# Probabilities turned in 32x32 blocks by VectorE and carried to their partitions by GpSimd's transfers through DRAM, in a two-layer hybrid diffusion backbone

## The reference

```python
h = modulate(rms_norm(x, g_mix[l]), sh1, sc1)          # hc: the same for the context tokens
a_b, a_c, a_x, na_q, na_k, na_v, sw_q, sw_k, sw_v, ga, gb, gc = split_in(h @ w_in[l])
o_a = a_b * short_conv(a_c * a_x, conv_w[l])
o_b = neighbourhood_attention(...)                     # 8 heads of 64, keys: latent + context, bias rpb
o_c = window_attention(...)                            # 8 query heads, 2 key heads, rotary, sink
x = x + gt1 * merge_branches((o_a, o_b, o_c), (ga, gb, gc), w_branch[l], w_out[l])
x = x + gt2 * expert_choice_ffn(modulate(rms_norm(x, g_ffn[l]), sh2, sc2), ...)   # 16 experts of 1024
```

## Time and profile before

| what | value |
|---|---|
| median of 3 runs | 1846.57 us (1845.81 to 1846.89) |
| span of the profiled execution | 1846.3 us |
| busy: PE, DVE, ACT, POOL | 1689.6, 771.0, 478.0, 111.4 us |
| mean granted TensorE clock | 0.976 |
| HBM read, written | 539.13 MB, 2.98 MB |

### The profile page before, as it was taken

The page is one execution under the profiler, slowest core; times in us unless marked ns, Lnnn a source line. Parts: engine busy times, 40 slices in busy tenths (PEclk is TensorE's granted clock), DMA queues, the critical chain, the costliest instruction groups (busy, mean ns, idle before and its releaser), DMA issues.

```text
span 1846.3 us, 26514 instructions
## 1 busy us (share of the span) xinstructions
PE 1689.6 (92%) x10854; PEld 977.2 (53%) x10854; DVE 771.0 (42%) x1746; ACT 478.0 (26%) x1052; POOL 111.4 (6%) x149
## 2 busy tenths in 40 slices
PE   5999999999998999999898799989999997777866
PEld 2887777777674333333232398877883332222222
DVE  3455556674434233333323665577753222111111
ACT  3324455552223100000000434465441000000001
POOL 1001210000001000000000101300001000000000
PEclk8999999999998999999999999999998999999998
DMA  9532322127778999999999764337899999999996
GB/s 353 154 91 69 106 72 80 35 81 256 251 286 326 409 428 427 428 428 428 427 429 426 271 206 133 96 115 252 282 364 385 426 426 426 426 425 426 426 426 281
DMA packets 152035, 543.83 MB, mean 295 GB/s; under 512 B 10026, under 2 KB 92400, under 8 KB 126700
## 3 DMA queue, kind: packets, MB, share of 16 engines
q1 hardware_dynamic: 149104, 535.35, 74.0%
q0 software_dynamic: 2400, 6.16, 1.2%
q10 hardware_dynamic: 412, 0.64, 0.1%
HBM read 539.13 MB, written 2.98 MB: 294 GB/s over the span
## 4 chain that ended last, share of the span: by engine, by line
PE 68%; DMA 23%; DVE 4%; ACT 2%; SPq 2%; issue 1%; POOL 0%; DVEq 0%; ACTq 0%
PE bank L2158 20%; PE bank L2019 12%; PE bank L2020 11%; PE bank L2021 11%; DMA ring<-in_w_exp_down 8%; DMA ring<-in_w_exp_gate 7%; DMA ring<-in_w_exp_up 4%; DMA spare<-in_w_exp_gate 3%; PE bank L2132 2%; PE bank L2048 2%; PE bank L2071 2%; PE bank L1934 2%; PE bank L2058 2%; PE bank L2187 1%; DMA ring<-in_w_ada 1%
## 5 line engine op out<-in xcount | busy, mean ns | idle before, releaser
L2158 PE MATMUL bank<-ring,XEP 128*32 128x256 f32 (+1 forms) x2384 | 384.9, 617 | 37.1 <-DMA ring<-in_w_exp_gate 20.7
L2019 PE MATMUL bank<-HH,WH 128*128 128x512 f32 (+1 forms) x864 | 312.1, 361 | 5.7 <-DVE HL L1627 4.7
L2020 PE MATMUL bank<-HL,WH 128*128 128x512 f32 (+1 forms) x864 | 300.4, 348 | 0.0
L2021 PE MATMUL bank<-HH,WL 128*128 128x512 f32 (+1 forms) x864 | 299.9, 347 | 0.0
L2158 PEld LDWEIGHTS bank<-ring,XEP 128*32 128x32 f32 (+1 forms) x2384 | 114.1, 130 | 277.5 <-issue 227.8
L1598 DVE TENSOR_TENSOR WL<-ring,WH 128x1024 fp32r<-128x1024 f32 (+1 forms) x172 | 185.0, 1078 | 133.4 <-ACT WH L1362 132.6
L1856 DVE TENSOR_TENSOR X<-X,bank 128x512 f32<-128x512 f32 x184 | 114.0, 682 | 188.2 <-PE bank L2187 100.0
L2019 PEld LDWEIGHTS bank<-HH,WH 128*128 128x128 f32 x864 | 163.8, 190 | 54.0 <-issue 25.9
L1362 ACT CAST WH<-ring 128x1024 fp32r<-128x1024 f32 (+1 forms) x172 | 158.0, 926 | 100.5 <-PE bank L2021 64.7
L2158 PE MATMUL bank<-ring,HIDT 128*32 128x256 f32 (+1 forms) x1232 | 153.6, 481 | 31.3 <-DMA ring<-in_w_exp_down 31.3
L2021 PEld LDWEIGHTS bank<-HH,WL 128*128 128x128 f32 x864 | 163.8, 190 | 21.2
(11 more groups left out here) (244 smaller groups left out, 1955.4 us busy)
## 6 DMA issues: line engine op xcount, KB each, us to landing
ring<-in_w_exp_gate SPq DMA_DIRECT2D x55, 2048.0 KB, 30.9
ring<-in_w_exp_up SPq DMA_DIRECT2D x49, 2048.0 KB, 34.4
ring<-in_w_exp_down SPq DMA_DIRECT2D x48, 2048.0 KB, 36.6
ring<-in_w_ada SPq DMA_DIRECT2D x48, 1024.0 KB, 7.4
ring<-in_w_in SPq DMA_DIRECT2D x40, 1024.0 KB, 6.3
split_slot<-in_w_exp_up SPq DMA_DIRECT2D x8, 2048.0 KB, 29.3
split_slot<-in_w_exp_down SPq DMA_DIRECT2D x8, 2048.0 KB, 33.5
ring<-in_w_in SPq DMA_DIRECT2D x28, 512.0 KB, 5.2
```

The source lines that it names most:

```text
L2019: mm(t, wh, hi[:, k, 0:b.n], start=k == 0, stop=False)
L2020: mm(t, wh, lo[:, k, 0:b.n], start=False, stop=False)
L2021: last = mm(t, wl, hi[:, k, 0:b.n], start=False, stop=k == b.kk - 1)
L2158: last = mm(out_bank[tw * g:tw * g + tw, 0:nw], stationary(k), w[:, g::G] if spread else w[:, nw * g:nw * g + nw], start=k == 0, stop=k == ...
```

## The change

TensorE's transposes of the probabilities and ScalarE's copies of them are gone, and the banks `TB` are not used any more. In their place:

- VectorE, right after it has normalised a unit, waits for its own result and turns `PB` in blocks of 32x32 into a tile `PBT` (one for both heads of a pair, at the end of the streaming ring). Ahead of the first head it waits until the pair before has left `PBT`.
- GpSimd, per pair, writes `PBT` to one of two DRAM buffers, waits for that write, waits for the values that last read the target, and issues four reads, each of which brings one quarter of the columns to 32 partitions of `PTL` or `PTC`, now in another order of dimensions.
- The streaming ring is 1,024 elements shorter while attention runs.
- Values run two pairs after the last pair of their set in layer 0 (at 0.4 of the pair's k-steps) and one pair after it in layer 1 (at 0.8). In stage C the first `dpair` has its steps in another order, with the last values further in.
- The bias steps of GpSimd are put in another place: a first one (layer 0) or two (layer 1) pairs' worth ahead, then one pair's worth, four transfers and two masks, behind each turn of a pair that has a bias.

The core of the diff:

```diff
+PBT_W = 1024
@@ def load
-            if self.top + size > STREAM[self.layer] * SLOT:
+            if self.top + size > STREAM[self.layer] * SLOT - self.kept:
@@ def attention
-                at_ = sorted(at_ + [(-(-per * 3 // 10), values), (-(-per * 7 // 10), lower)], key=lambda a: a[0])
+                at_ = sorted(at_ + [(-(-per * (8 if last else 4) // 10), lambda: values(pair[0].pair - (1 if last else 2))), (-(-per * (10 if last else 8) // 10), lower)], key=lambda a: a[0])
@@ values, turn
-            for st in P.turned:
-                P.add("pv", set=st)
-            P.lower += P.turned
-            P.turned = []
+            while P.turned and P.turned[0].end <= until + 1:
+                P.add("pv", set=P.turned[0])
+                P.lower.append(P.turned.pop(0))
-            for x in pair:
-                P.add("turn", unit=x)
-                if x.end:
-                    P.turned.append(x.set)
+            P.add("turn", pair=pair)
+            if pair[1].end:
+                P.turned.append(pair[1].set)
@@ stage C, for d2 in range(4)
-            run(atoms[:1 + KD // 2])
-            values()
-            run(atoms[1 + KD // 2:1 + KD])
-            lower()
-            run(atoms[1 + KD:mid])
+            if d2 == 0:
+                mid = 2 * KD + 3
+                atoms = atoms[:KD + 2] + atoms[KD + 8:2 * KD + 9] + atoms[KD + 2:KD + 8] + atoms[2 * KD + 9:]
+                done = 0
+                for n in (KD + 1, 2 * KD)[-len(P.turned):]:
+                    run(atoms[done:n])
+                    values(P.turned[0].end - 1)
+                    run(atoms[n:n + 3])
+                    lower()
+                    done = n + 3
+                run(atoms[done:mid])
+            else:
+                run(atoms[:mid])
@@ after the plan of a layer
-        P.steps[l] = out
+        P.steps[l] = bias_order(out, 2 * (l + 1))
+def bias_order(steps, ahead):
+
+    due = [s for s in steps if s.kind == "bias"]
+    out = []
+
+    def pair():
+
+        now = [due.pop(0) for _ in range(2)] if due else []
+        out.extend(now + [Step(kind="mask", layer=s.layer, unit=s.unit) for s in now])
+
+    for s in steps:
+        if s.kind == "bias":
+            if s.unit.u == min(t.unit.u for t in steps if t.kind == "bias"):
+                for _ in range(ahead // 2):
+                    pair()
+            continue
+        out.append(s)
+        if s.kind == "turn" and s.pair[0].bias:
+            pair()
+    assert not due
+    return out
@@ buffers
+        bounce = [nc.dram_tensor(f"bounce{i}", (128, PBT_W), f32, kind="Internal").ap() for i in range(2)]
-        PTL = sb("PTL", [128, 2, 4, SEQ], R_PT)
-        PTC = sb("PTC", [128, 2, 2, SEQ], R_PT + 8192)
+        PTL = sb("PTL", [128, 8, 2, 4, 32], R_PT)
+        PTC = sb("PTC", [128, 8, 2, 2, 32], R_PT + 8192)
+        PBT = [[sb(f"PBT{l}{nk}", [128, 4, 2, nk, 32], R_RING + 16384 * STREAM[l] - 4 * PBT_W) for nk in (4, 2)] for l in range(DEPTH)]
@@ gpsimd
+                    elif s.kind == "mask":
+                        mask(s.unit)
+                    elif s.kind == "turn":
+                        x = s.pair[1]
+                        pool.wait_ge(turn_ready, x.u + 1)
+                        run, held = 16 * x.nk // 32, bounce[x.pair % 2]
+                        if x.pair > 1:
+                            pool.wait_ge(pt_in, 64 * (x.pair - 1))
+                        pool.dma_start(held[:, 0:4 * run], PBT[l][x.set.grp][:].rearrange("p b h c j -> p (b h c j)")).then_inc(pt_out, 16)
+                        pool.wait_ge(pt_out, 16 * (x.pair + 1))
+                        if x.set.pt_before:
+                            pool.wait_ge(pv_ready, x.set.pt_before)
+                        j = x.qt % 2
+                        for b in range(4):
+                            blocks = bass.AP(tensor=held.tensor, offset=held.offset + run * b, ap=[[PBT_W, 32], [32 * PBT_W, 4], [1, run]])
+                            turned = (PTL, PTC)[x.set.grp][32 * b:32 * b + 32, 4 * j:4 * j + 4].rearrange("p a h c j -> p a (h c j)")
+                            pool.dma_start(turned, blocks).then_inc(pt_in, 16)
@@ scalar
-                    elif kind == "turn":
-                        x = s.unit
-                        act.wait_ge(turn_ready, x.u + 1)
-                        if x.set.pt_before:
-                            act.wait_ge(pv_ready, x.set.pt_before)
-                        nc.scalar.copy(buf[:, x.hh, :, 128 * j:128 * j + 128],
-                                       TB[x.u % 2][:, 0:128 * nk].rearrange("p (k q) -> p k q", k=nk)).then_inc(pt_ready, 1)
@@ vector, after the scaling
+                        dve.wait_ge(norm_ready, x.u + 1)
+                        if x.hh == 0 and x.pair:
+                            dve.wait_ge(pt_out, 16 * x.pair)
+                        turned = PBT[l][x.set.grp][:, :, x.hh, :, :].rearrange("p b c j -> p c b j")
+                        nc.vector.transpose(turned, PB[u2][:, 0:n].rearrange("p (c b j) -> p c b j", b=4, j=32)).then_inc(turn_ready, 1)
@@ tensor
-                    elif kind == "turn":
-                        x = s.unit
-                        pe.wait_ge(norm_ready, x.u + 1)
-                        if x.u >= 2:
-                            pe.wait_ge(pt_ready, x.u - 1)
-                        for c in range(x.nk // 128):
-                            last = nc.tensor.transpose(TB[x.u % 2][:, 128 * c:128 * c + 128], PB[x.u % 2][:, 128 * c:128 * c + 128], IDENT)
-                        last.then_inc(turn_ready, 1)
@@ tensor, values
-                        pe.wait_ge(pt_ready, st.end)
+                        pe.wait_ge(pt_in, 64 * st.end)
-                                last = mm(PVB[64 * hh:64 * hh + 64, 0:SEQ], v, buf[:, hh, c, :], start=c == 0, stop=c == n - 1,
+                                last = mm(PVB[64 * hh:64 * hh + 64, 0:SEQ], v, buf[:, :, hh, c, :], start=c == 0, stop=c == n - 1,
```

More of the change, by code:

```diff
@@ L205, in __init__ @@
         self.occupants = []
-        self.units = self.sets = self.biases = 0
+        self.units = self.sets = self.biases = self.pairs = 0
+        self.kept = 0
         self.mods = 0
@@ L502, in open_tile @@
             b.tile = P.tile(**kw)
+        P.kept = PBT_W
         ch = col_chunk("nv")
@@ L556, in attention @@
                     pair = []
+                    n = P.pairs
+                    P.pairs += 1
                     for hh in range(2):
                         x = Step(br=br, p=p, hh=hh, qt=2 * st.grp + j, u=P.units, info=info, nk=TOK if st.grp == 0 else CTX, set=st,
-                                 end=hh == 1 and j == 1, bias=None, layer=l)
+                                 end=hh == 1 and j == 1, bias=None, layer=l, pair=n)
                         P.units += 1
-                        st.end = P.units
+                        st.end = P.pairs
                         if br == "na" and x.qt < 2:
```

27 lines of the change are left out of this document (6 added, 21 removed).

## The result

| kernel | median of runs | span profiled | granted clock |
|---|---|---|---|
| before | 1846.2 us (4 runs, 1843.4 to 1846.9) | 1846.3 us | 0.976 |
| after | 1901.9 us (4 runs, 1894.6 to 1903.4) | 1901.6 us | 0.956 |

The ratio is 1.0296, with a 95% interval from 1.0276 to 1.0315. The forecast was 1822 us and its range ended at 1852. It went the way of rival (b), which had 0.18, and further than the 1865 us priced there.

The account below looks back on a forecast made before the run. Attention was taken as bound by TensorE, the expert stage by the weight stream. Terms of 10 + 9 + 5 + 4 - 2 = 26 us gave 1820.6 us, put at 1822, with a range of 1802 to 1852.

Parts of the forecast that it names:

- rival (b): na branches: GpSimd's serial chain sets the periods; landings longer by 1.5 us cost 44.5 us, giving 1865; chance 0.18.
- sw: 6.3 a pair, 11.8 a double, hidden in both layers: Window branches: the turn holds GpSimd 6.3 us a pair, 11.8 per large and small pair, and costs no time.
- a chain of 9.3: Each large pair: 9.3 us from the end of VectorE's transpose to the landed last read, 6.3 + about 3.
- the co-bound: Layer 1 sw: VectorE at 9.5 us a pair against TensorE's 9.6, so 4 us gained of a possible 8.8.
- wrong, if writes land in over 5 us: GpSimd's bounce writes: expected at 3 to 4.5 us; landings over 5 us would mean a slower kernel.
- both medians: Argument against slower na periods: bias landings had medians of 2.4 us in layer 0 and 2.9 in layer 1.
- Values of layer 0 come 14 to 15 us after it: Layer 0: values come 14 to 15 us after VectorE's transpose, so 5 us are spare.
- the later values at a loss of 2 us, and the ring at nothing: Layer 1's last values ten k-steps later, with two expert loads: -2 us; shorter ring delays some loads, costing nothing.
- layer 1's 15.5 + 7: Layer 1, TensorE's ceiling: 15.5 us of transposes and 7 us of waits for the probabilities go.
- Rival (d): Layer 1: weight stream, already held by its rate, ends when it did despite shorter TensorE work; 1843 to 1847; chance 0.07.
- (a): Whole kernel: nothing stalls, TensorE keeps 44 to 46 us, 1801; chance 0.2.
- the signs named: Profile: VectorE over 90% in layer 1 sw; TensorE idle ahead of values in layer 1 na, nowhere in layer 0 sw.

Follow-up runs that it names:

- e12: The kernel before without TensorE's transposes and ScalarE's copies, values computed from a tile filled with zeros once a layer: 1809.2 us, ratio 0.9795.
- e15: e12 with the streaming ring shorter: 1812.3 us, ratio 0.9815 to the kernel before.
- e5: The changed kernel without the transfers and without VectorE's transposes, values waiting for the scaled probabilities: 1824.9 us, ratio 0.9888 to the kernel before.
- e3: The changed kernel without the transfers; values wait for VectorE's transposes alone and read a zero-filled tile: 1831.7 us, ratio 0.9930 to the kernel before.
- e13: e3 with all bytes of the bounce moved, reads fetching other data into DRAM, values not waiting for them: 1842.8 us, ratio 0.9977 to the kernel before.
- e9: The change in layer 0 alone, with the last head pair of the window branch left to TensorE: 1839.3 us, ratio 0.9960 to the kernel before.
- e6: The kernel before with the streaming ring 1,024 elements shorter during attention, nothing else: 1848.7 us, ratio 1.0016.
- e16: e12 with the values one or two pairs later, as in the changed plan: 1824.3 us, ratio 0.9871 to the kernel before.
- e11: The changed kernel with layer 1's modulation weights for its first nine chunks cut to an eighth: 1887.0 us, ratio 1.0224 to the kernel before.

## Why the prediction was wrong

Put one behind the other, the medians account for the whole way:

| step | us | predicted |
|---|---|---|
| turns and copies away (before to e12) | -36.7 | -46.5 |
| shorter ring (e15) | +3.1 | 0 |
| values later, and the plan around them (e5) | +12.6 | 2 |
| VectorE's transposes (e3) | +6.8 | 8 |
| the bytes alone (e13) | +11.1 | 0 |
| the waits for them (after) | +59.1 | 11 |
| sum | +56 | -26 |

(The predicted column sorts the prediction's terms: VectorE was to eat 3 us in layer 0's sw and 4.8 in layer 1's, GpSimd 2 in layer 0's na and some 9 in layer 1's na. Its sum is 26 within rounding.)

By stage, from the profiled executions, against the terms of the prediction's sum (na from the first na score to the first sw score, sw from first to last score; minus is faster; the last column is what the waits for the transfers added):

| stage | predicted | before to after | e13 to after |
|---|---|---|---|
| layer 0 na | -10 | -7.4 | +5.4 |
| layer 0 sw | -9 | -1.3 | +7.2 |
| layer 0 hand-over | 0 | +15.5 | +14.3 |
| layer 1 na | -5 | +10.7 | +14.1 |
| layer 1 sw | -4 | +31.9 | +20.9 |
| layer 1 hand-over | +2 | +6.8 | +3.4 |
| sum | -26 | +56.2 | +65.3 |

**The step that failed: "sw: 6.3 a pair, 11.8 a double, hidden in both layers".** It set the time that the turn holds GpSimd against the period of a pair, a question of rate. What the window branch needs is a question of delay: by the prediction's own count the values come 1.1 pairs after the transpose, and at the 9.6 us wanted per pair that is 10.6 us against a chain of 9.3, the same one to two us of slack as in layer 1's na, for which alone it was worked out. The 9.3 was too short as well, in layer 1 by 3 to 4 us. From the end of VectorE's second transpose of a pair to its last landed read the trace has, in the median of each branch, 10.3 and 9.6 us in layer 0 (na, sw) and 12.8 and 13.4 in layer 1; the eight pairs of layer 1's sw lie between 8.8 and 16.6, seven of them over 11.

Not all of the 31.9 us there are this wait. Without any transfer the branch was already longer than before: from first to last score it took 74.7 us before, 68.9 without turns (e12), 73.1 with the shorter ring (e15), 77.5 with the later values (e5), 82.8 with VectorE's transposes (e3), 85.7 with the bytes (e13) and 106.6 in the change. So the saving of 4 us was lost before the waits came on top. Nor was VectorE the co-bound that the prediction made of it (9.5 of 9.6 us a pair): in e3 it was busy 71.7 of 89.2 us there, 80%, and TensorE idled 11.1 us. 11.6 us of TensorE's idle in all of e3 are the wait for `QT` shown above, which no term of the prediction has.

**Second: the chain had medians in it, and the engine that waits pays the tails.** The values wait for one write and then for the slowest of four reads. The write was assumed at 3.8 us and measured at 3.6, so "wrong, if writes land in over 5 us" was the wrong test: the median never did. But writes took up to 8.8 us and reads up to 7.8, and a wait is not regained where TensorE is the bound. Rival (b) had the longer landings right. It priced a mean delay d over the time that GpSimd is held in layer 0's na, where the large writes landed in 2.9 us in the median, and in layer 1's na; the window branches and the hand-over of layer 0, where 42 of the 65 us between e13 and the change are, are not in it. Its own argument against itself, "both medians", was what misled.

**Third: what a stall does besides.** TensorE's direct waits for reads are 41.8 us, the cost of waiting 59.1. The profiled executions of e13 and of the change lie 65.5 us apart. The sums over all stretches from the first score to the first gather of both layers hold 65.3 of them, e13 first, then the change (us, then busy times):

```profile
sum 698.60, PE 658.84 PEld 498.99 DVE 472.45 ACT 283.13 POOL 204.12; mean PE 131.77 PEld 99.80 DVE 94.49 ACT 56.63 POOL 40.82
```
```profile
sum 763.90, PE 679.37 PEld 507.40 DVE 472.41 ACT 282.89 POOL 199.41; mean PE 135.87 PEld 101.48 DVE 94.48 ACT 56.58 POOL 39.88
```

TensorE idled 84.5 us instead of 39.8, 44.8 more, nearly all of it the direct waits. And the same matmuls kept it busy 20.5 us longer: the granted clock was 0.85 in the window branch of layer 1 instead of 0.94, and 0.93 in layer 0's hand-over instead of 0.98. Eight sets of sixteen values matmuls behind waits took 3.06 to 3.68 us instead of 1.95; they are 13 of the 20.5, and the other products have the rest. The prediction had no such term, since the clock stood at 1.00 in all stretches of the earlier trace rows. Two waits of other engines for the same chain are in the trace too: in the window branch of layer 1 GpSimd twice waited, 14.7 us in all, for the values to leave the single `PTL`, and VectorE waited 20.8 us over the whole kernel for `PBT`, 17.7 of them in layer 0.

**Fourth: the hand-over of layer 0.** "Values of layer 0 come 14 to 15 us after it": within attention 12.6 us were lost against e13 all the same (255.8 against 243.2). One reason shows in GpSimd's timeline: its bias steps stood ahead of them in the queue, and so four of the first sixteen writes began 5 to 10 us after VectorE's transposes. At its end there is no next pair, SP had loads of 1 MB under way, and the write landed after 8.84 us. The hand-over cost 14.3 us more than without the waits (190.4 against 176.1), and e9 does not have this loss.

**Fifth: the later values at a loss of 2 us, and the ring at nothing.** The ring costs 3 (by twelve runs of e6; the 3 of e15 alone are within the noise). The move costs 7 us with the turns in place and 12 to 15 without. In layer 0 it is all in the hand-over (172.7 to 179.2), where the order of the steps changed; 5.1 us of these 6.5 are TensorE's busy time, 165.1 to 170.2 us at a granted clock of 0.99 and 0.95, and in e3 and e13, with the same order, only 3 of the 6.5 are there. In layer 1 it is mostly in attention (159.6 to 166.1, e16). Why it costs twice as much with the turns gone is only partly settled: the rotary wait above explains 4 us of it.

**What held.** VectorE's turn was taken at 0.69 and 0.42 us and is 0.711 and 0.444. Its cost came in layer 1, where 4.8 us of a possible 8.8 were forecast: 6 to 8 us measured, of which 5.3 in sw (77.5 to 82.8, e5 to e3). The 3 us forecast for layer 0's sw did not come. The Trainium skill, VectorE: DVE Perf Modes, section The three transpose paths, would have made 1.24 us of its bf16 figure, an estimate; the trace is far below, at 0.711 in f32. Layer 0's saving of 24 us was 23.4 in the profiled execution of e12; of layer 1's 15.5 + 7, only 15.5 came. The 7 were TensorE's idle time in layer 1, all of which the ceiling counted as gone; without turns 4.8 us of it were left against 6.5 before. The values' operand in runs of 32 elements costs nothing: 379 ns in e3 as in e12. The bytes cost 11 us, where the prediction had nothing for them, and the expert stage is as long as before. Rival (d) did not happen, nor (a), which was below even the ceiling. Of the signs named, two failed: VectorE was to be over 90% busy in layer 1's sw and was at 64%, and TensorE was to idle ahead of values nowhere in layer 0's sw and did so three times, 8.5 us with the end of attention. The issue of a bounce transfer took 0.55 to 0.56 us in the median, less than the 0.615 assumed, with VectorE busier than before. The Trainium skill's rule that VectorE's two-port modes hold up GpSimd's descriptors (SBUF — State Buffer, section Who interferes with whom) would show as long issues; the longest here are 584 ns for the writes and 742 ns for the reads, so there is little of it.

## What to carry to other kernels

- When work is moved off the bounding engine by way of another queue, work out two numbers: how long the queue is held (rate) and how long it is from the last input to the landed result (delay), and set the second against the time to where it is due, for every stage by itself, the ends of loops above all. Take the tail of the landings under the traffic of that stage, not the median, above all where several transfers must all have landed.
- Kernels that keep a transfer's bytes and drop its wait, and ones that keep the wait and cut the bytes, tell rate from delay in two runs. Here the bytes were worth 11 us and the wait 59.
- Let the slow path do only those parts that have slack, and leave the last one ahead of a hand-over on the direct path: e9 is the same change on 28 of 48 pairs, and turns +3.0% into -0.4%.

## What the runs showed of the hardware

- One transfer of 512 KB from 128 partitions to DRAM, issued by GpSimd, landed in 2.9 to 8.8 us: medians 2.9 in layer 0's na branch (DMA share 0.54), 3.5 in its sw (0.62), 3.6 in layer 1's na (0.57), 4.1 in layer 1's sw (0.74). With SP's loads in layer 1 made lighter (e11), the median of layer 1 fell from 3.9 to 3.3. The Trainium skill, DMA: Bandwidth & Descriptors, section Anatomy of one DMA — SWDGE (gpsimd) path, fits 2.0 us and bytes / 436e3, which is 3.2 us for this size, an estimate: it comes near the quiet landings here (2.9) and says nothing of the loaded ones.
- VectorE's block transpose of 128x512 f32 from SBUF to SBUF takes 711 ns and of 128x256 444 ns, hardly more than the copy of as many elements in the earlier trace rows (691 ns).
- A stall costs TensorE twice: after the wait of 3.60 us that ended at 1286.47, its granted clock was 0.50 for the next sixteen matmuls, which took 1.73 us more than at full clock (3.68 against 1.95). After the wait of 1.95 us that ended at 1200.68 they took 1.95. From e13 to the change TensorE was busy 20.5 us longer with the same matmuls, on top of 44.8 us more idle.
